# Wide up projection with a summed low half, in a two-layer hybrid decoder trunk

## The reference, cut to what matters

```python
proj = h @ w_in[i]                                   # 352 of its columns are MLA's latents
...
h = rms_norm(x, ffn_norm[i])
u = causal_depthwise_conv(h @ w_up[i], conv_w[i], conv_b[i])   # 1024 -> 2 * 2816
x = x + (silu(u[..., :D_FF]) * u[..., D_FF:]) @ w_down[i]      # 2816 -> 1024
x = x + (p[i] @ ple_proj[i]) * sigmoid(x @ ple_gate[i])
```

## Time and profile before

| what | us |
|---|---|
| median of 3 runs (lowest, highest) | 695.11 (695.02, 696.01) |
| the profiled execution, its own time | 695.29 |
| its span | 693.5 |
| TensorE busy in the span | 679.1 |
| ScalarE, GpSimd, VectorE busy | 397.2, 392.0, 347.7 |

### The profile page before, as it was taken

The page is one execution under the profiler, slowest core; times in us unless marked ns, Lnnn a source line. Parts: engine busy times, 40 slices in busy tenths (PEclk is TensorE's granted clock), DMA queues, the critical chain, the costliest instruction groups (busy, mean ns, idle before and its releaser), DMA issues.

```text
span 693.5 us, 11414 instructions
## 1 busy us (share of the span) xinstructions
PE 679.1 (98%) x4452; PEld 614.0 (89%) x4452; DVE 347.7 (50%) x574; ACT 397.2 (57%) x582; POOL 392.0 (57%) x214
## 2 busy tenths in 40 slices
PE   7999999999999999999999999999999999999997
PEld 5988988799999999998879889878999999999985
DVE  5867867745333333335268587666363333333333
ACT  5669774665555555555364787746655555555542
POOL 5423201159888888887820132013798877777781
PEclk9999999999999999999999999999999999999999
DMA  9951232655555555553395421154555555555411
GB/s 316 382 189 61 65 118 74 228 183 181 184 189 189 190 188 189 193 190 102 103 320 187 142 92 70 62 182 126 181 184 184 185 188 191 191 190 191 163 30 61
DMA packets 74436, 115.05 MB, mean 166 GB/s; under 512 B 2336, under 2 KB 58272, under 8 KB 74144
## 3 DMA queue, kind: packets, MB, share of 16 engines
q1 hardware_dynamic: 73248, 111.75, 48.1%
q10 hardware_dynamic: 1152, 2.81, 1.1%
HBM read 113.51 MB, written 1.05 MB: 165 GB/s over the span
## 4 chain that ended last, share of the span: by engine, by line
PE 86%; DVE 5%; ACT 4%; SPq 1%; DMA 1%; POOL 1%; issue 1%; DVEq 0%; ACTq 0%
PE ps L897 24%; PE ps L898 23%; PE ps L899 23%; PE ps L986 2%; PE ps L1023 2%; PE ps L911 1%; DVE wl L1510 1%; DMA ukv<-w_ukv 1%; PE ps L1006 1%; PE ps L977 1%; PE ps L951 1%; PE ps L1016 1%; SPq L348 1%; POOL wl L438 1%; DVE wl L1779 1%
## 5 line engine op out<-in xcount | busy, mean ns | idle before, releaser
L438 POOL TENSOR_TENSOR wl<-raw,wh 128x2048 fp32r<-128x2048 f32 (+1 forms) x72 | 324.5, 4539 | 87.3 <-ACT wh L565 87.3
L565 ACT ACTIVATE wh<-raw 128x2048 fp32r<-128x2048 f32 (+1 forms) x102 | 185.6, 1828 | 113.3 <-PE ps L899 107.4
L897 PE MATMUL ps<-hT_h,wh 128*128 128x256 f32 x752 | 213.8, 284 | 0.4 <-DVE wl L1510 0.3
L898 PE MATMUL ps<-hT_l,wh 128*128 128x256 f32 x752 | 212.8, 283 | 0.0
L899 PE MATMUL ps<-hT_h,wl 128*128 128x256 f32 x752 | 212.8, 283 | 0.0
L897 PEld LDWEIGHTS ps<-hT_h,wh 128*128 128x128 f32 x752 | 144.2, 192 | 2.5 <-DVE wl L1510 1.1
L898 PEld LDWEIGHTS ps<-hT_l,wh 128*128 128x128 f32 x752 | 144.3, 192 | 0.8
L899 PEld LDWEIGHTS ps<-hT_h,wl 128*128 128x128 f32 x752 | 144.2, 192 | 0.0
L1811 DVE SCALAR_TENSOR_TENSOR pb<-ps,conv,pb 128x255 f32<-128x255 f32 (+1 forms) x96 | 39.7, 476 | 109.2 <-ACT pb L832 109.0
L425 POOL TENSOR_SCALAR st<-st 128x2 f32<-128x2 f32 (+3 forms) x26 | 9.3, 360 | 148.1 <-ACT lat L624 74.6
L1811 DVE SCALAR_TENSOR_TENSOR pt<-ps,conv,pt 128x255 f32<-128x255 f32 (+1 forms) x80 | 33.1, 476 | 97.3 <-ACT pt L832 97.1
(11 more groups left out here) (270 smaller groups left out, 935.7 us busy)
## 6 DMA issues: line engine op xcount, KB each, us to landing
raw<-w_up SPq DMA_DIRECT2D x44, 1024.0 KB, 5.1
raw<-w_down SPq DMA_DIRECT2D x22, 1024.0 KB, 4.9
raw<-w_in SPq DMA_DIRECT2D x16, 1024.0 KB, 9.1
raw<-w_o SPq DMA_DIRECT2D x6, 1024.0 KB, 4.9
raw<-ple_gate SPq DMA_DIRECT2D x6, 1024.0 KB, 4.9
raw<-w_in SPq DMA_DIRECT2D x4, 704.0 KB, 5.3
ng<-norm_gains ACTq DMA_DIRECT2D x2, 1024.0 KB, 6.5
raw<-w_o SPq DMA_DIRECT2D x4, 512.0 KB, 3.6
```

The lines of the kernel that those rows point to most:

```text
L438: pool.tensor_tensor(wl[:, slot, 0:n], raw[:, slot, 0:n], wh[:, u % RING, 0:n].bitcast(F32), ALU.subtract).then_inc(ffn_l_made, 1)
L565: act.activation(wh[:, u % RING, c:n], raw[:, slot, c:n], ACT.Copy).then_inc(h_made, 1)
L897: pe.matmul(dst, a_h, b_h, start=start, stop=False, skip_group_check=True)
L898: pe.matmul(dst, a_h, b_l, start=False, stop=False, skip_group_check=True)
```

## The change

- **Up.** `hT_h` and `hT_l` become the two halves of one tile `hT_hl` (for each block k 256 high columns and 256 low ones beside them). The stationary high weight streams both halves in one matmul of 512 columns, and the low weight streams the high half in one of 256. So a block takes two matmuls in place of three, and each column group j has a bank of its own: columns 0 to 255 hold two of the passes, columns 256 to 511 the third. All four banks 4 to 7 are used in every step. up(s) now waits, for each half, for the conv of the same half of step s-1.
- **Sum.** For each half of a step ScalarE copies the upper columns of its two banks to SBUF (`up_l`, in the space of `hT`), and VectorE adds them to the lower columns, in PSUM (`up_summed`). Only then come tap2 and the taps, half by half.
- **ScalarE's order** in a step becomes: copy of half 0, `high` of the next A (steps 0 and 1: of the next B), two tap2, copy of half 1, two tap2, `high` of the next B (from step 2 on), silu, `high` of the next D (step 0: A of step 2), the wait for the product, `gT_h`. The first of these `high` in step 0 is that of A of step 1.
- **Second layer's unit B of MLA** is split in two parts during the gate of the first layer: ScalarE rounds it into `pt_r`, VectorE subtracts into `wl`. TensorE then takes it in three passes of float32r.
- ScalarE and VectorE split the first two quarters of the second layer's turned x before they wait for the last quarters. The squares of x in the first layer move within the same order.

The core of the diff:

```diff
@@ ScalarE, mlp @@
-                    bank = 4 + 2 * par
-                    high(u, turn)
-                    high(u + 1, turn)
-                    if not (isinstance(s, int) and s < 2):
+                    early = isinstance(s, int) and s < 2
+                    if isinstance(s, int) and s < 1:
+                        high(u, turn)
+                    if not early:
                         act.wait_ge(F["g_low"], base["g_low"] + s - 1)
                     for half in range(2):
                         unit_done(act, layer, this + half, turn)
+                        if not (isinstance(s, int) and s < 1):
+                            act.wait_ge(F["up_summed"], base["up_summed"] + (s - 1) * 2 + half + 1)
+                        act.activation(up_l[:, 2 * half:2 * half + 2, :],
+                                       ps[:, 4 + 2 * half:6 + 2 * half, SEQ:512], ACT.Copy
+                                       ).then_inc(F["low_half"], 1)
+                        if half == 0:
+                            high(u + early, turn)
+                        act.wait_ge(F["up_summed"], base["up_summed"] + s * 2 + half + 1)
                         for j in range(2):
...
+                    if not early:
+                        high(u + 1, turn)
                     act.wait_ge(F["conv_done"], base["conv_done"] + s * 4 + 2)
                     act.activation(cv[par][:, 0:2, :], cv[par][:, 0:2, :], ACT.Silu
                                    ).then_inc(F["silu"], 1)
+                    high(u + 2, turn)
                     act.wait_ge(F["prod"], base["prod"] + s + 1)
...
-                    if not (isinstance(s, int) and s < 1) and not down_early:
-                        high(u + 2, turn)
@@ TensorE, latents of the second layer, unit B @@
+                        if lows:
+                            mm = pe.matmul(o, hT_l[:, k, tok], pt_r[:, c], start=False,
+                                           stop=k == KT - 1, skip_group_check=True)
+                        else:
+                            pe.matmul(o, hT_h[:, k, tok], pt_r[:, c], start=False, stop=False,
+                                      skip_group_check=True)
+                            pe.matmul(o, hT_h[:, k, tok], wl[:, M_MLA_B, c], start=False,
+                                      stop=False, skip_group_check=True)
@@ TensorE, up @@
+                        if not (isinstance(s, int) and s < 1):
+                            pe.wait_ge(F["conv_done"], base["conv_done"] + (s - 1) * 4 + 2 * half + 2)
...
                             for k, c in enumerate(cols):
-                                mm = split_product(o, wh[:, high, c], wl[:, slot, c],
-                                                   hT_h[:, k, :], hT_l[:, k, :], k == 0,
-                                                   k == KT - 1)
+                                pe.matmul(ps[:, bank, :], wh[:, high, c],
+                                          hT_hl[:, k].rearrange("p a n -> p (a n)"),
+                                          start=k == 0, stop=False, skip_group_check=True)
+                            for k, c in enumerate(cols):
+                                mm = pe.matmul(ps[:, bank, 0:SEQ], wl[:, slot, c], hT_h[:, k, :],
+                                               start=False, stop=k == KT - 1,
+                                               skip_group_check=True)
@@ VectorE, mlp @@
+                    for half in range(2):
+                        pair = slice(2 * half, 2 * half + 2)
+                        dve.wait_ge(F["low_half"], base["low_half"] + s * 2 + half + 1)
+                        up_s = ps[:, 4 + 2 * half:6 + 2 * half, 0:SEQ]
+                        tt(up_s, up_s, up_l[:, pair, :], ALU.add).then_inc(F["up_summed"], 1)
...
@@ during the first layer's gate: ScalarE, then VectorE @@
+                    act.activation(pt_r[:, 0:COLS[M_MLA_B]], raw[:, M_MLA_B, 0:COLS[M_MLA_B]],
+                                   ACT.Copy).then_inc(F["mla_high"], 1)
...
+                    tt(wl[:, M_MLA_B, 0:n], raw[:, M_MLA_B, 0:n], pt_r[:, 0:n].bitcast(F32),
+                       ALU.subtract).then_inc(F["mla_low"], 1)
```

More of the change, by code:

```diff
@@ L640, in _ @@
                 if layer:
+                    x_high(0, AT_START, (0, 1))
                     act.wait_ge(F["x_done"], 4 * layer)
                     x_square(3).then_inc(F["x_squared"], 1)
-                x_high(0, AT_START)
+                    x_high(0, AT_START, (2, 3))
+                else:
+                    for t in range(TT):
+                        act.wait_ge(x_landed[t], 16)
+                        for half in range(2):
+                            x_square(2 * t + half).then_inc(F["x_squared"], 1)
+                    act.dma_start(pos_i[:], positions).then_inc(pos_landed, 16)
+                    x_high(0, AT_START)
                 high(M_SB_Q, halves=True)
@@ L832, in mlp @@
                             act.activation(cv[par][:, 2 * half + j, :],
[L833 to L837, removed]
-                        high(u + 2, turn)
+                                           ps[:, 4 + 2 * half + j, 0:SEQ],
+                                           ACT.Identity, bias=conv[:, 3, f], scale=conv[:, 2, f]
+                                           ).then_inc(F["tap2"], 1)
+                    if not early:
+                        high(u + 1, turn)
                     act.wait_ge(F["conv_done"], base["conv_done"] + s * 4 + 2)
@@ L1277, in _, with up @@
                 x_T(hn, AT_MIDDLE, ("hn_ready", 0), free="pp_ready")
-                def up(s, par, u, turn=0, first=False):
+                def up(s, u, turn=0, first=False):
                     for half in range(2):
                         slot, high = unit(u + half, turn)
-                        if half == 0:
-                            if not (isinstance(s, int) and s < 1):
-                                pe.wait_ge(F["conv_done"], base["conv_done"] + (s - 1) * 4)
+                        if not (isinstance(s, int) and s < 1):
+                            pe.wait_ge(F["conv_done"], base["conv_done"] + (s - 1) * 4 + 2 * half + 2)
                         for j in range(2):
-                            o = ps[:, 4 + 2 * par + half, j * 256:(j + 1) * 256]
+                            bank = 4 + 2 * half + j
                             cols = [slice(k * 256 + j * P, k * 256 + (j + 1) * P)
@@ L1296, in up @@
                                         pe.wait_ge(F["xT_high"], base["xT_high"] + 7 + k // 4)
-                                    pe.matmul(o, wh[:, high, c], hT_h[:, k, :], start=k == 0,
-                                              stop=False, skip_group_check=True)
-                                    pe.matmul(o, wl[:, slot, c], hT_h[:, k, :], start=False,
-                                              stop=False, skip_group_check=True)
+                                    pe.matmul(ps[:, bank, 0:SEQ], wl[:, slot, c], hT_h[:, k, :],
+                                              start=k == 0, stop=False, skip_group_check=True)
                                 for k, c in enumerate(cols):
@@ L1801, in mlp @@
                 def mlp(s, par):
-                    bank = 4 + 2 * par
-                    for tap, name, before in ((1, "tap1", "tap2"), (0, "conv_done", "tap1")):
-                        d = 2 - tap
-                        for i in range(4):
-                            half, j = divmod(i, 2)
-                            f = bass.ds(s * 2 + (half * FT + j), 1)
-                            o = cv[par][:, i, d:SEQ]
-                            dve.wait_ge(F[before], base[before] + s * 4 + (2 * half + 2 if tap else i + 1))
-                            stt(o, ps[:, bank + half, j * 256:j * 256 + SEQ - d],
-                                conv[:, tap, f], o, ALU.mult, ALU.add).then_inc(F[name], 1)
+                    for half in range(2):
+                        pair = slice(2 * half, 2 * half + 2)
+                        dve.wait_ge(F["low_half"], base["low_half"] + s * 2 + half + 1)
+                        up_s = ps[:, 4 + 2 * half:6 + 2 * half, 0:SEQ]
+                        tt(up_s, up_s, up_l[:, pair, :], ALU.add).then_inc(F["up_summed"], 1)
+                        dve.wait_ge(F["up_summed"], base["up_summed"] + s * 2 + half + 1)
+                        for tap, name, before in ((1, "tap1", "tap2"), (0, "conv_done", "tap1")):
+                            d = 2 - tap
+                            for i in (2 * half, 2 * half + 1):
+                                f = bass.ds(s * 2 + (half * FT + i - 2 * half), 1)
+                                o = cv[par][:, i, d:SEQ]
+                                dve.wait_ge(F[before], base[before] + s * 4 + i + 1)
+                                stt(o, ps[:, 4 + i, 0:SEQ - d], conv[:, tap, f], o, ALU.mult,
+                                    ALU.add).then_inc(F[name], 1)
                     dve.wait_ge(F["silu"], base["silu"] + s + 1)
```

57 lines of the change are left out of this document (39 added, 18 removed).

## The result

The changed kernel takes 715.33 us in the median of 4 runs (713.91 to 716.12), against 695.32 for the kernel before (695.02 to 696.01, 4 runs): ratio 1.0286, 95% interval 1.0273 to 1.0298. It is slower, as forecast, but by 20 us and not 8, and outside the range. The profiled execution took 713.91 us, its span is 712.1 (before 695.29 and 693.5), and the mean granted clock of TensorE over it is 0.987 (before 1.0). It is the fastest of the four, and the profile accounts for its time, not for the 1.4 us that the median lies above it. Of the later kernels x3_gfirst, x5_bfirst and x8_split_before had one or two executions in a slow state (751.86 to 3840.68 us), which the ratios leave out; without them these medians would be lower by 0.1 to 0.2.

The account below looks back on a forecast made before the run. TensorE was taken as the bound (busy 679.1 of 693.5 us). Per layer -4.3 - 0.3 + 3.5 + 5.5 = +4.4; two layers +8.8, unit B -0.8, together +8.0: 703.3 profiled, median 703.0, range 694 to 712.

Parts of the forecast that it names:

- Matmuls of up: TensorE's up: pairs at 0.348, a step saves 0.39 and is 16.60, eleven steps save 4.3 us a layer.
- Copy 0.60, sum 0.69 and not held: Per half, ScalarE's copy 0.60 and VectorE's PSUM addition 0.69, not made to wait for a GpSimd `low` to end.
- First chain: up(2) waits for step 1's conv, queued behind step 0's held remainder: +3.5 us a layer; today's 0.3 wait goes.
- Second chain: down(10) waits for step 10's remainder, after held product and held remainder: 5.5 us late in each layer.
- Unit B: Second layer's MLA unit B in three passes: 24 matmuls at 0.160 for 16 records totalling 4.6 us, saving 0.8.
- T: The end of up(10), the time from which the chain to down(10) is counted.
- What a gap costs: TensorE's gaps ahead of up(2) and down(10), priced at their length: 3.5 and 5.5 us a layer.
- The loop between: Loop steps between the chains: drift of 0.1 to 0.2 a step into a reserve of about 2, taken as 0.
- The ring: Loop cycle: two GpSimd `low`, held remainder, sums, tap2, taps, B's `high`; 16.7 us against TensorE's 16.6.
- the forecast's -3.1: Forecast change of the stretch from down(0) to down(8), in us for each layer.
- the ring binds: Rival, 0.11: GpSimd, VectorE and ScalarE set the pace; at 17.1 a step 3.0 more a layer, 711.
- one of the holds slips: Rival, 0.11: product or remainder issued 0.5 us after a `low` began might get in; 694 to 698.

Follow-up runs that it names:

- x3_gfirst: Changed kernel with ScalarE's `high` of u+2 (the down weight's copy) put back behind `gT_h` in every step; 697.12 us, ratio 1.0028.
- x5_bfirst: x1_fill with 8 fillers ahead of down(10) and the next B's `high` directly behind the copy of half 1; 697.68 us, ratio 1.0029.
- x8_split_before: Kernel before with each GpSimd `low` in two pieces of at most 1024 columns, nothing else; 695.63 us, ratio 1.0000.
- x1_fill: Changed kernel with matmuls whose results nobody reads in both gaps (15 ahead of up(2), 25 ahead of down(10)); 709.10 us, ratio 1.0195.
- x7_nosum: Changed kernel without the copy, the addition and their waits, leaving out the up product's third pass; 695.35 us, ratio 0.9991.
- x4_order: Kernel before with only the `high` of u+2 moved ahead of the wait for the product; 700.62 us, ratio 1.0074.
- x2_split: Changed kernel with each GpSimd `low` in two pieces of at most 1024 columns; 688.76 us, ratio 0.9914.

## Why the prediction was wrong

Point by point:

- *Matmuls of up.* Right. A loop step without a wait is 16.61 in seven of these kernels (16.60 forecast). Before it was 16.98 and not 16.99, so a step saves 0.37 and not 0.39.
- *Copy 0.60, sum 0.69 and not held.* Right: 44 sums, 689 ns in the mean, though a `low` ran at the start of 43.
- *First chain.* Right in place and cause. In the second layer, where the clock stayed full, MLP to down(0) is +2.28 against +2.0.
- *Second chain.* Right in place and cause, +5.9 against +5.5. The product ends at T + 11.8 and the remainder at T + 16.8, forecast T + 11.3 and T + 16.4. The 0.4 to 0.5 come in with half B's sum and tap2. The sum ends at T + 3.6 and its two tap2 at T + 4.8, where I had T + 3.2 and T + 4.2.
- *Unit B.* Right, -0.89 against -0.8.
- *What a gap costs.* This step failed. "TensorE starts up(2) at 162.5 and not 159.0: 3.5 us" and "down(10) is 5.5 late" price a gap at its length. Behind three of four gaps the clock was halved for 6.8, 6.8 and 3.4 us. A down's matmul then takes 0.427 and not 0.227, and 2.67 + 1.95 + 1.37 = 6.0 us are lost (x1_fill). With the 0.3 by which down(10) to the transposes is longer at full clock too it is 6.3 against the kernel before, for which the forecast had nothing.
- *The loop between.* This step failed too: "It drifts by 0.1 to 0.2 a step into a reserve of about 2, so I take 0". The ring measures 17.11 us. GpSimd's first `low` of steps 9 and 10 starts at 300.18 and 317.29, against my 16.7. The terms that were short are the two tap2 behind a sum, 1.20 and 1.19 for my 0.9 and 1.0; the others came within 0.1. So each step drifts by 0.5 and not by 0.1 to 0.2, and from up(7) on TensorE feels it. 1.9 a layer of the forecast's -3.1 are missing, 3.8 in all: 1.7 a layer is the ring (x5_bfirst), 0.2 the smaller saving of the matmuls.

These close the account: 8.0 + 6.3 + 3.8 = 18.1, and the two chains were 0.3 and 0.4 longer than forecast in each layer, another 1.4 less the 0.65 by which the execution reached the first MLP earlier: 18.8 against 18.7 in the span. The 1.4 that the median lies above the profiled execution has no profile. The other three executions have mean clocks of 0.985 and 0.986 for its 0.987, which would fit a longer stretch at half clock, but isn't shown. The rival "the ring binds" was held to be another case, at 0.11. It came true beside the forecast, at 1.7 a layer where it gave 3.0. The rival "one of the holds slips" is refuted: every product or remainder issued 0.47 after a `low` began was held, and in x3_gfirst one issued 0.05 after it. The range of 694 to 712 treated the cases as alternatives, and none had a price for the clock.

The Trainium skill, "Trainium Architecture — The Big Picture", What this means for kernel authors, calls the port pair that VectorE and GpSimd share an exclusive lock and not a split of bandwidth. The trace agrees, with 4.69 us for an instruction of 0.69, and 2.48 when the other engine's instruction was half as long. The Trainium skill, "TensorE: Matmul & The Clock Gate", What's actually happening, describes half of the clock as the state that TensorE falls back to without recent activity. The trace agrees, with 0.50 behind three gaps, though behind the fourth it is 1.00. I had used that page of the Trainium skill in the prediction for the cost of a matmul and not for this.

What stays open is which gaps cost the clock. Gaps of 3.63 us from start to start stand ahead of up(2) in both layers, and one of them did; gaps of 2.77 in the profiled execution of x7_nosum did and in x4_order did not, and of the other executions of x7_nosum five had room for one such fall at most. Between the two gaps ahead of up(2) the rows show no other difference than the time at which the gap falls, and I didn't vary that by itself.

## What to carry to other kernels

When an instruction can be held by another engine, ask what is queued behind it and who waits for that. Defer it behind the work that TensorE needs next, to a time at which the other engine is idle if there is one. If it can't be deferred, cut the holding instruction into pieces. Price a gap of 2.4 us or more in TensorE's stream as its length plus a possible 1.4 to 2.7 us at half clock behind it (what it cost here where the clock fell), and test whether two small changes meet in one chain before adding their prices. A ring that is estimated within 0.1 of a step is no slack: write it down with the delay from one engine's end to the next one's start, from rows in which the same kind of memory is written.

## What the runs showed of the hardware

- A VectorE instruction with two SBUF inputs that is issued during a GpSimd subtraction ends 0.55 after that subtraction, however early it came: 5.13 us for a product that starts 0.05 after it (x3_gfirst), 4.69 for those at 0.47, 2.83 for those at 2.35 (x5_bfirst), 2.48 for those at 0.47 with pieces of 1024 columns (x2_split). An addition with one input in PSUM took 0.69 on all 44 occasions.
- ScalarE starts 0.18 us after VectorE has written PSUM (sum to 311.01, tap2 at 311.19), and 0.03 to 0.04 after it has written SBUF (product to 322.45, `gT_h` at 322.49).
- At 1.2 GHz a matmul of 512 columns starts every 0.427 us and at 2.4 GHz every 0.227 (down(10) of the changed kernel, across the rise of the clock), a ratio of 1.88 and not 2.
